# Forgetting attention: one query block's division placed ahead of the next block's maxima, and the copies of the transposed weights shared between ScalarE and VectorE

## The reference

```python
bounds = [(0, N_META)] + [(N_META + i * Q_BLOCK, N_META + (i + 1) * Q_BLOCK) for i in range(n_blocks)]
for s0, s1 in bounds:
    logits = (jnp.einsum('bhqd,bhkd->bhqk', q[:, :, s0:s1], k[:, :, :s1]) * scale
              + cum[:, :, s0:s1, None] - cum[:, :, None, :s1])
    causal = jnp.arange(s1)[None, :] <= jnp.arange(s0, s1)[:, None]
    probs = jax.nn.softmax(jnp.where(causal, logits, -jnp.inf), axis=-1)
    outs.append(jnp.einsum('bhqk,bhkd->bhqd', probs, v[:, :, :s1]))
```

## Time and profile before

| what | value |
|---|---|
| median of 3 runs | 1637.6 us (1633.4 to 1639.91) |
| the profiled execution, its own time | 1641.7 us |
| its span on the core | 1640.0 us |
| PE matmul busy in the span | 1570.8 us, 96% |
| VectorE busy | 880.3 us, 54% |
| ScalarE busy | 669.5 us, 41% |
| mean granted TensorE clock | 0.973 |

### The profile page before, as it was taken

The page is one execution under the profiler, slowest core; times in us unless marked ns, Lnnn a source line. Parts: engine busy times, 40 slices in busy tenths (PEclk is TensorE's granted clock), DMA queues, the critical chain, the costliest instruction groups (busy, mean ns, idle before and its releaser), DMA issues.

```text
span 1640.0 us, 38874 instructions
## 1 busy us (share of the span) xinstructions
PE 1570.8 (96%) x16218; PEld 1468.4 (90%) x16218; DVE 880.3 (54%) x1479; ACT 669.5 (41%) x1077; POOL 150.2 (9%) x275
## 2 busy tenths in 40 slices
PE   7997999999999999999999999998999999999998
PEld 6997888899789999999999899955579999999886
DVE  5689644433556666666333333355445666666222
ACT  5443133333545444443223466365535444444111
POOL 1457085300000000000000000000000000000000
PEclk9998999999999999999999999987799999999999
DMA  5221100000123333333232222230013333333331
GB/s 149 66 65 55 30 17 4 3 4 4 30 78 90 90 90 90 90 90 104 81 106 71 61 81 77 79 106 1 1 41 102 90 90 90 90 90 95 103 105 69
DMA packets 210747, 113.63 MB, mean 69 GB/s; under 512 B 8032, under 2 KB 207410, under 8 KB 210642
## 3 DMA queue, kind: packets, MB, share of 16 engines
q1 hardware_dynamic: 210034, 109.93, 23.1%
q10 hardware_dynamic: 608, 2.16, 0.4%
HBM read 109.95 MB, written 2.13 MB: 68 GB/s over the span
## 4 chain that ended last, share of the span: by engine, by line
PE 84%; DVE 8%; ACT 4%; issue 2%; SPq 1%; DMA 0%; ACTq 0%; DVEq 0%
PE BK L676 82%; PE BK L1187 2%; ACT XB L1245 1%; DVE ALL L1720 1%; DVE WLO L1713 1%; DVE ALL L1713 1%; DVE SS L2321 1%; ACT L1245 1%; ACT ALL L1245 1%; ACT WHI L1245 1%; SPq L394 0%; DVE PB L1713 0%; DVE ALL L1717 0%; DVE MQA L1713 0%; DVE U L2174 0%
## 5 line engine op out<-in xcount | busy, mean ns | idle before, releaser
L1713 DVE TENSOR_TENSOR WLO<-RAW,WHI 128x1024 fp32r<-128x1024 f32 (+1 forms) x182 | 239.8, 1318 | 158.4 <-ACT WHI L1245 157.4
L1245 ACT ACTIVATE WHI<-RAW 128x1024 fp32r<-128x1024 f32 (+1 forms) x182 | 202.6, 1113 | 241.7 <-PE BK L676 241.6
L676 PE MATMUL BK<-YNH,WHI 128*128 128x264 f32 (+1 forms) x1216 | 250.9, 288 | 1.3 <-DVE CUM L1717 1.3
L676 PE MATMUL BK<-YNH,WLO 128*128 128x264 f32 (+1 forms) x1216 | 248.3, 286 | 0.0
L676 PE MATMUL BK<-YNL,WHI 128*128 128x264 f32 (+1 forms) x1216 | 247.2, 285 | 0.0
L676 PE MATMUL BK<-XNH,WHI 128*128 128x258 f32 (+1 forms) x1056 | 219.1, 289 | 13.2 <-DVE WLO L1713 9.7
L676 PE MATMUL BK<-XNH,WLO 128*128 128x258 f32 (+1 forms) x1056 | 215.5, 286 | 0.0
L676 PE MATMUL BK<-XNL,WHI 128*128 128x258 f32 (+1 forms) x1056 | 214.7, 285 | 0.0
L676 PEld LDWEIGHTS BK<-YNH,WHI 128*128 128x128 f32 x1216 | 191.3, 189 | 2.9 <-DVE CUM L1717 1.6
L676 PEld LDWEIGHTS BK<-YNH,WLO 128*128 128x128 f32 x1216 | 189.2, 189 | 0.0
L676 PEld LDWEIGHTS BK<-YNL,WHI 128*128 128x128 f32 x1216 | 188.6, 189 | 0.0
(11 more groups left out here) (293 smaller groups left out, 2255.5 us busy)
## 6 DMA issues: line engine op xcount, KB each, us to landing
RAW<-in_ffn_w_up_dram SPq DMA_DIRECT2D x88, 512.0 KB, 3.9
RAW<-in_ffn_w_down_dram SPq DMA_DIRECT2D x32, 704.0 KB, 4.6
RAW<-in_odd_w_in_dram SPq DMA_DIRECT2D x24, 512.0 KB, 3.9
RAW<-in_even_w_in_dram SPq DMA_DIRECT2D x22, 512.0 KB, 3.9
CB<-cum_dram SPq DMA_DIRECT2D x8, 528.0 KB, 8.1
RAW<-in_even_w_out_dram SPq DMA_DIRECT2D x8, 512.0 KB, 3.8
RAW<-in_odd_w_out_dram SPq DMA_DIRECT2D x8, 512.0 KB, 3.8
XIN<-in_x_dram ACTq DMA_DIRECT2D x4, 512.0 KB, 5.3
```

The source lines that it names most:

```text
L676: return pe.matmul(o, l, r, start=start, stop=stop, skip_group_check=check)
L1245: return nc.scalar.activation(o, i, f, **kw)
L1713: return nc.vector.tensor_tensor(o, x, y, op)
```

## The change

Two edits, both in attention.

First, VectorE divides block 3 before it takes block 4's maxima: `weights(t)` comes ahead of `maxima(t + 1)` where `j` is `NQ - 2`. For all other blocks it stays behind.

Second, ScalarE's `out_pt(t)` copies only the first head's transposed weights. A new function on VectorE, `second_head(t)`, copies those of the second head. It is issued for every step directly after the maxima and the division, and before `low`. It waits for `fx_t` (the transposes of this very step) and, at block 0, for `fx_o` of the pair before. It raises a new semaphore `fx_pt1`, for which PE's `turn` and `mix` wait beside `fx_pt`. Line numbers behind line 1172 move by 1 to 23.

```diff
--- before.py
+++ after.py
@@ -1170,6 +1170,7 @@
                     i, j = divmod(t, NQ)
                     if t:
                         pe.wait_ge(S("fx_pt"), t)
+                        pe.wait_ge(S("fx_pt1"), t)
                     else:
                         pe.wait_ge(S("fx_vs"), 7)
                     lo, n = TILES[j]
@@ -1195,6 +1196,7 @@
                         if i:
                             pe.wait_ge(S("x_lo"), x_ready["out1"] - KD + i)
                     pe.wait_ge(S("fx_pt"), NQ * i + (NQ if b else 3))
+                    pe.wait_ge(S("fx_pt1"), NQ * i + (NQ if b else 3))
                     blocks = [k for k in range(NQ) if TILES[k][0] < HT * (b + 1)]
                     for k in blocks:
                         lo = max(TILES[k][0], HT * b)
@@ -1672,9 +1674,9 @@
                     if j == 0 and i:
                         act.wait_ge(S("fx_o"), i)
                     if j:
-                        fn(PTT[:, :, 1:j + 1, lo:n], BK[:, 4:6, 0:P * j].rearrange("p e (k t) -> p e k t", t=P), ACT.Copy)
-                    meta = BK[0:N_META, 4:6, 512 - P:512 - P + w] if j < NQ - 1 else BK[0:N_META, 6:8, HT:HT + P]
-                    fn(PTT[0:N_META, :, 0, lo:n], meta, ACT.Copy).then_inc(S("fx_pt"), 1)
+                        fn(PTT[:, 0, 1:j + 1, lo:n], BK[:, 4, 0:P * j].rearrange("p (k t) -> p k t", t=P), ACT.Copy)
+                    meta = BK[0:N_META, 4, 512 - P:512 - P + w] if j < NQ - 1 else BK[0:N_META, 6, HT:HT + P]
+                    fn(PTT[0:N_META, 0, 0, lo:n], meta, ACT.Copy).then_inc(S("fx_pt"), 1)
 
                 def out(i):
 
@@ -2334,6 +2336,20 @@
                         pr = PR[0:w, t % BUFS, e, 0:n]
                         ts(pr, pr, RC[0:w, j, e:e + 1], None, ALU.mult).then_inc(S("fx_d"), 1)
 
+                def second_head(t):
+
+
+                    i, j = divmod(t, NQ)
+                    lo, n = TILES[j]
+                    w = n - lo
+                    ve.wait_ge(S("fx_t"), t + 1)
+                    if j == 0 and i:
+                        ve.wait_ge(S("fx_o"), i)
+                    if j:
+                        ve.tensor_copy(PTT[:, 1, 1:j + 1, lo:n], BK[:, 5, 0:P * j].rearrange("p (k t) -> p k t", t=P))
+                    meta = BK[0:N_META, 5, 512 - P:512 - P + w] if j < NQ - 1 else BK[0:N_META, 7, HT:HT + P]
+                    ve.tensor_copy(PTT[0:N_META, 1, 0, lo:n], meta).then_inc(S("fx_pt1"), 1)
+
                 def low(i):
 
                     ve.wait_ge(S("ot_hi"), i + 1)
@@ -2342,9 +2358,14 @@
                 maxima(0)
                 for t in range(FOX_TILES):
                     i, j = divmod(t, NQ)
+
+                    if j == NQ - 2:
+                        weights(t)
                     if t + 1 < FOX_TILES:
                         maxima(t + 1)
-                    weights(t)
+                    if j != NQ - 2:
+                        weights(t)
+                    second_head(t)
                     if j == 1 and i:
                         low(i - 1)
                 low(FOX_PAIRS - 1)
```

## The result

The changed kernel takes 1658.28 us in the median of 4 runs (1654.98 to 1662.01), the kernel before 1638.76 in the same comparison (4 runs). The ratio is 1.0123, with a 95% interval from 1.0083 to 1.0163: slower by 20 us. The forecast was 1655, with a range of 1642 to 1671 and a chance of 0.82 for slower.

What follows compares the result with a forecast made beforehand. PE's waits, chiefly 1.45 us a pair for block 3's division, and the low clock behind them bound attention. Steps of +14.9 us plus 2 for the clock gave 17 more: median 1655, range 1642 to 1671.

Steps and rivals of the forecast that it cites:

- 1: Block 0's to block 1's transposes: 4.13 us against 3.57 before, +0.56, VectorE's copy waiting for the old value product.
- step 2: Block 1's to block 2's transposes: 3.42 us against 2.18, +1.24, with `low` and block 3's maxima behind block 1's copies.
- 3: Block 2's to block 3's transposes: 2.23 us against 2.61, -0.38, all that is left of the gain aimed at.
- step 4: Block 3's transposes to the value product: 1.89 us against 1.76, +0.13, the product waiting for block 4's maxima.
- Step 5: Value product and block 1's scores, up to block 4's transposes: 3.77 us, unchanged.
- The sixth: Block 4's to block 0's transposes: 3.86 us against 3.29, +0.57, with maxima and division behind VectorE's copies.
- The clock term: PE's clock in attention: one low stretch a pair kept, 2 us added for further stretches, between bounds 0 and about 18.
- Rival 1: Attention's clock no longer falls, no single wait being as long as 1.45 us: about 1635, no change; chance 0.12.
- Rival 2: The clock falls a second time in each pair, around block 1's transposes: 18 us more, 1670; chance 0.11.
- rival 3: VectorE's copies find their transposes done, so the 1.45 us wait and low clock go: about 1608; chance 0.05.
- Rival 4: VectorE's and ScalarE's PSUM reads hinder each other, 0.4 us more at each of four blocks: 1668; chance 0.04.

Runs made afterwards that it cites:

- runs with added reciprocals: Only block 3's division moved ahead of block 4's maxima, with block 3's reciprocal computed three or six more times: 1621.97 and 1637.99 us.
- the division alone: Kernel before with only block 3's division moved ahead of block 4's maxima, all copies left on ScalarE: 1612.35 us, ratio 0.9827.
- the division alone with three more reciprocals: The division alone, with block 3's reciprocal computed three more times before the division: 1621.97 us, ratio 0.9903 to the kernel before.
- block 4 shared: The division alone, with only block 4's second head copied by VectorE, behind the next block 0's division: 1609.90 us, ratio 0.9813.
- 6 more: The division alone, with block 3's reciprocal computed six more times before the division: 1637.99 us, ratio 0.9992 to the kernel before.

## Why the prediction was right

**What bounds the kernel.** Confirmed: the 1.45 us wait for the division and the low clock behind it. The runs with added reciprocals show both. The second is the larger: 0.6 us a pair for the wait, and 3.0 for the clock (17.1 to 17.2 against 14.12 with waits of the same sum and the clock up).

**Step by step.** Two pairs are shown: the third, which has the one low stretch that the prediction assumed (1119.9 to 1126.7), and the seventh, the pair above, at the full clock throughout.

| step | worked out | third pair | seventh pair | seventh, from, to |
|---|---|---|---|---|
| 1 | 4.13 | 4.14 | 4.13 | 1184.34 to 1188.47 |
| 2 | 3.42 | 3.53 | 3.53 | 1188.47 to 1192.00 |
| 3 | 2.23 | 2.15 | 2.15 | 1192.00 to 1194.15 |
| 4 | 1.89 | 1.95 | 1.94 | 1194.15 to 1196.09 |
| 5 | 3.77, low clock | 3.74 | 2.09 | 1196.09 to 1198.18 |
| 6 | 3.86, low clock | 4.19 | 3.10 | 1198.18 to 1201.28 |
| pair | 19.3 | 19.70 | 16.94 | |

Where the clock did what was assumed, all steps but the sixth are right within 0.11 us. The sixth is 0.33 over, for a reading that was wrong. Its ten transposes were put at 1.93 us as their price at the low clock, but in the earlier trace rows they run from 1132.87 to 1134.80, and the low stretch ends at 1134.2. In the third pair they lie wholly within it:

```profile
1123.56 2.33 PE L1188 MATMUL BK<-IDENT,PR 128*16 128x128 f32 x10
```

That is 2.33 against 1.25 us at the full clock (1198.18 above), a factor of 0.54 and not 0.71. Step 5 gains alike, 3.74 against 2.09. So of the two prices that the prediction gave a low stretch, 1.65 and 2.85, the second was nearly right: 2.8 (19.70 less 16.94).

**The clock term** is the one that was wrong. The prediction kept one low stretch of 6.7 us in each pair and added 2 us. Measured were 47.8 us at the low level, in six stretches from 3.4 to 13.7 us, over the first five pairs, and none in the last three. What it costs can be estimated. Eight pairs of 16.94 and 1 us for the ends (as in the division alone: 109.2 less 8 times 13.52) are 136.5; attention took 152.4, so 16 us. For the kernel before no pair at the full clock exists. Its waits have the same sum as those of the division alone with three more reciprocals, 14.12 a pair, so about 114 in all and 25 us for the clock. By this account the change lengthened the chain by 22.7 us, and lost 9.5 less to the clock. My account was 15 and +2. The totals agree (13.2 in the profiled execution, 20 in the medians, 17 forecast); the split does not. The main part of that difference is in step 4. Its length was right, but its +0.13 compares with transposes that ran at the low clock (1.76); at the full clock, where they take 1.03, it is +0.9. So the chain was worked out rightly, the clock was assumed, and that the total came within 3 us is in part luck.

**The rivals.** Rival 1, that the clock no longer falls, was true of the last three pairs: 16.94 us lies in the 16.45 to 17.65 that it gives. Rival 2, by which a pair takes 21.5, was in effect true of the second and fourth pairs (23.2 and 21.6 us, with 17 and 13.7 us at the low level). The measured time lies between the two. The price of rival 3, 1608, is close to that of the division alone, 1612, and of block 4 shared, 1610: there no copy of VectorE's stands still ahead of a due maximum. For the kernel as changed, step 2 spoke against it, and rightly. Rival 4: ScalarE's reads of PSUM didn't slow VectorE's. The 128x512 copy took 691 ns beside ScalarE's just as in the earlier trace rows.

**Signs named.** The waits ahead of block 3's transposes (1.0 expected, 0.99), block 1's (0.5, 0.39), block 4's scores (1.2, 1.27) and the value product (0.9, 0.91) are as named. The distance of 19 us between block 0's transposes holds for the third pair (19.7) and on average over the first six intervals (19.2), and for no other pair. Three signs failed. VectorE waits for the transposes or the value product in 32 steps, not in all 40: in block 3's eight the transposes are done by then. ScalarE's waits for PE's transposes are shorter, not longer, 34.3 us against 46.8. And "wrong if pairs stay at 17 us" is met to the letter by the last three pairs, 16.94 us. It was a poor sign, since it took the clock as given: these pairs are 2.8 us longer than one of 14.12, with the old sum of waits and the clock up.

**What stays open:** which mixture of waits and products lowers the clock. In the division alone, 0.60, 0.26 and 0.34 did not; in the changed kernel, waits of 0.8 to 1.3 did in five pairs and did not in three. The executions of the changed kernel differ among themselves by 7 us, and their granted clocks with them: 0.976 in the two of 1655 us, 0.971 and 0.970 in those of 1661 and 1662. Which pairs it fell in was looked at only in one. Why it fell in some pairs and not in others of the same length and the same waits is open.

## What to carry to other kernels

An instruction that waits for another engine blocks everything behind it on its own queue. Work moved to an idle engine must go where its wait is already over, behind what the others need next: against the division alone, the same copies cost 46 us in one place and 12 in the other. And test two edits apart: here one gained 29 us and the other took 46 away. Where TensorE's clock falls in a regular stage, look for the wait just ahead of the fall; here 0.6 us less of it gave back 3.6 us a pair.

## What was not expected of the hardware

The size of the clock's share. 0.6 us less of waits in a pair of 17.18 us took the low clock from 54.6 us of attention to none, and the time from 1641 to 1612. And it comes in degrees: with 3 more reciprocals 17 us at the low level, with 6 more 54.6. The kernels with six reciprocals more and before the change also drew to the same pair of 17.1 us. Their waits are split differently (1.16 and 0.30, against 1.45) but come to the same sum, so they don't tell whether the time would follow a small change of it.
